# Activation parts and the work buffers behind them start 32 bytes higher in SBUF, at 96 instead of 64 modulo 256

## The chip, the cores and the metric

One NeuronCore of a Trainium2 chip runs one program that holds two transformer-like blocks in a row. The metric is the device time of one execution in microseconds. Three timed executions of the kernel before stand against the same number of the changed one.

## The reference, cut to what matters

The input x is 256 tokens by 1024 features, with a context of the same shape. The first block scales and shifts a normalised x and ctx by learned modulations, runs gated linear attention in both directions with states carried from the context, projects back, and adds a gated feed-forward layer of width 2816. The second block projects its modulated input to a gated delta rule branch (8 heads, chunks of 64) and a chunked band attention branch (16 heads), merges them through gates, and ends with layer norms and another gated feed-forward layer with a short convolution. All of it is float32:

```python
hc = modulate(rms_norm(x, norm_g), shift, scale)
y = (silu(hc @ w_gate) * (hc @ w_up)) @ w_out          # first block's feed-forward, width 2816
proj = h @ w_in                                        # second block: 9232 columns
merged = gate_a * (o_a @ w_branch_a) + gate_b * (o_b @ w_branch_b)
x = layernorm(ALPHA * x + gate_t * (merged @ w_o), ln1_g, ln1_b)
```

Nearly all of the work is in such products of the 256 tokens with weight matrices of 1024 or 2816 rows.

## The kernel before, in words

The weights are laid out as 178 panels of 128 partitions x 2048 numbers. SyncE streams them in halves of 128x1024 through the six slots of `raw` (L140, issue at L295 to L298). A panel of kind "S" is multiplied on TensorE in three passes: ScalarE rounds a half of it to the upper part `w_hi` (`upper_half`, L946), VectorE subtracts that from the half to get the lower part `w_lo` (`lower_half`, L1460), four slots each. The activations are split in the same way into `act_hi` and `act_lo` (16 tiles of 128x256), and the hidden layer of the feed-forwards into `hidden_hi` and `hidden_lo` (22 tiles). Panels of other kinds are reduced on VectorE (L1493) or multiplied once by a padded vector (L451).

`three_pass` (L394 to L401, its matmul is L399) takes a weights pair and a moving pair and issues upper x upper, upper x lower, lower x upper, each with a load of 128 stationary columns and a stream of 256 (in two panels 512) moving columns:

```python
for p, (a, b) in enumerate(((a_hi, b_hi), (a_hi, b_lo), (a_lo, b_hi))):
    ins = pe.matmul(out_, a, b, start=start and p == 0, stop=stop and p == 2,
                    skip_group_check=True)
```

Here `a` is loaded as the stationary operand and `b` streams. A column panel (`quarter`, `panel`) loads slices of `w_hi`/`w_lo` and streams a 256-token tile of the activations, so each product reads 512 bytes of weights and 1024 bytes of activations in every partition. A token panel (`token_quarter`, for the values of both attentions) swaps the roles: 128 tokens of the activations are loaded and 256 columns of the weights stream. `project_hidden` does the same as a column panel from the hidden parts. In the trace's names the moving operand stands first: `panel_banks<-act_hi,w_hi` streams `act_hi`.

The order of work is written out by hand for each engine: a list of layers (`LAYERS`) gives the stream of panels, and for the delta rule and the band attention a table (`FILL`) says how many quarters of panels TensorE puts between their steps. Semaphores tie the engines: `landed` (DMA), `upper_ready`, `parts_ready`, `multiplied`, `panel_evacuated`. SyncE's queue waits for the release of a slot of `raw` before it issues the next load.

SBUF is allotted in the order of the declarations, each buffer at a multiple of 32 bytes. The start of each, modulo 256: `raw`, `w_hi`, `w_lo` and `x_t` 128 (the first of them at 16512), `columns` 128, `ident`, `ones`, `twice_diag` and `c_wide` 0, `mod_cols` 0, `rs` 160, `w_beta_a` 96, then at L169

```python
sb("act_home", [P, 48])
with ExitStack() as scope:
    hhi = sb("act_hi", [P, 16, T], F32R, scope)
    hlo = sb("act_lo", [P, 16, T], F32R, scope)
```

`act_home` starts at 128 modulo 256, is used by nothing and takes 192 bytes, so that `act_hi` starts at 64 modulo 256. All buffers behind it have sizes that are multiples of 256 bytes up to the last, so `act_lo`, `band_q`, `band_k` (which lie over the same place later), the work areas `gla_work`, `mix_work` and `ffn_work` with all their parts of 256 or more numbers, `hidden_hi` and `hidden_lo` start at 64 too. Every tile of 256 columns and every weight slice of 128 columns steps by a multiple of 256 bytes, so within a product the start modulo 256 is that of its buffer.

Of the kernel before, what the change touches and what calls it, by code (L numbers as in the profile page):

```python
# [21 lines left out]
P = 128  # L22
# [96 lines left out]
def two_blocks(nc, panels, x, ctx_x, columns, c_rows, w_glr, w_gate, w_beta_a, head_rows, rel_bias, out):  # L119
# [3 lines left out]
    with ExitStack() as ctx:  # L123
        def sb(name, shape, dt=F32, scope=ctx):
            return scope.enter_context(nc.sbuf_tensor(name, shape, dt))
# [40 lines left out]
            return cols[:, COL[name] + i:COL[name] + i + n]  # L166


        sb("act_home", [P, 48])  # L169
        with ExitStack() as scope:  # L170
            hhi = sb("act_hi", [P, 16, T], F32R, scope)
            hlo = sb("act_lo", [P, 16, T], F32R, scope)
# [1970 lines left out]
```

How the kernel before makes its waits and increments, by code:

```python
        @block.sync  # L285
        def _(sp):
            for u in range(2 * len(stream)):
                if u >= RAW:
                    kind, i = stream[(u - RAW) // 2]
                    if kind != "R":
                        sp.wait_ge(S(RELEASE[kind]), 2 * i + u % 2 + 1)
                    else:
                        for g in range(4):
                            sp.wait_ge(S(f"rows{g}"), 2 * i + u % 2 + 1)
                sp.dma_start(raw[:, u % RAW], panels[u // 2][:, u % 2 * HALF:u % 2 * HALF + HALF])\
                    .then_inc(S(f"landed{u % RAW}"), 16)
            for k in (0, 2, 4, 6):
                sp.wait_ge(S("out_ready"), k + 2)
                sp.dma_start(out[:, k:k + 2], f_out[:, k:k + 2]).then_inc(S("out_stored"), 16)
            sp.wait_ge(S("out_stored"), 64)
# [2 lines left out]
        @block.gpsimd  # L303
# [3 lines left out]
            def step(ins):  # L307
                made[0] += 1
                ins.then_inc(S("constants"), 1)
                pool.wait_ge(S("constants"), made[0])
# [34 lines left out]
            assert made[0] == CONSTANTS, made[0]  # L345
            for g in range(4):
                for d in range(2):
                    pool.dma_start(wgp[32 * g + 16 * d:32 * g + 16 * d + 16, 512 * d:512 * d + 512], w_gate[d])\
                        .then_inc(S("gate_w_landed"), 16)
            pool.wait_ge(S("h1_lo"), KT)
            step(pool.memset(resets, 1.0))
            step(pool.memset(resets.rearrange("p (a b) -> p a b", b=T)[:, :, 0], 0.0))
```

## Time and profile before

| what | value |
|---|---|
| three timed executions | 1027.47, 1031.45, 1030.05 us; median 1030.05 |
| the profiled execution's own time | 1027.39 us |
| its span, first to last instruction | 1025.6 us |
| TensorE busy | 948.5 us (92%), 8438 matmuls |
| VectorE busy | 702.4 us (68%), 1112 instructions |
| ScalarE busy | 547.6 us (53%), 829 instructions |
| mean granted TensorE clock | 0.966 |
| HBM read | 194.43 MB, 191 GB/s over the span |

The span of the profiled execution is 1.8 us shorter than its own time. Busy times of TensorE are those of overlapping products, so the share says that something is always in flight, not how quickly products follow each other. The granted clock is the share of 2.4 GHz that TensorE was given; it is 1.0 or 0.5 in a stretch.

### The profile page before, as it was taken

The page shows a single profiled execution, that of the slowest core. Times are in us where ns is not written, and L with a number is a line of the kernel's source. Part 1 is how long each engine was busy: PE and PEld are TensorE (multiplying, and loading weights), DVE is VectorE, ACT ScalarE, POOL GpSimd, SP SyncE. Part 2 cuts the span into 40 slices and gives each one's busy share as a digit, 9 for nine tenths or more (in the row PEclk, how much of TensorE's full clock was granted, in tenths as well). Part 3 has the DMA queues.
Part 4 walks back from the last instruction along what each step waited for, and adds up shares of the span by engine and source line. Part 5 has one row for each costly group of instructions (what it writes and reads, how often), then busy time and mean ns, then how long its engine had stood idle before and what let it go on. Part 6 is the DMA issues. An engine that isn't in the chain of part 4 may idle for free.

```text
span 1025.6 us, 19911 instructions
## 1 busy us (share of the span) xinstructions
PE 948.5 (92%) x8438; PEld 895.5 (87%) x8438; DVE 702.4 (68%) x1112; ACT 547.6 (53%) x829; POOL 26.7 (3%) x71
## 2 busy tenths in 40 slices
PE   4699999979999998899899999989998699999995
PEld 1489999869999998799689998978998599999994
DVE  2659837677787775888784544456668689989744
ACT  2668232655544445665726335366764467766434
POOL 2100000000000000400100000000000000000000
PEclk9899999979999999899999999989999899999997
DMA  9825656537888887357324335544356635666921
GB/s 337 298 90 161 236 200 211 201 124 250 308 282 286 301 281 246 101 180 257 120 84 166 116 134 134 185 134 135 114 204 219 224 113 195 193 198 192 340 88 41
DMA packets 57401, 196.78 MB, mean 192 GB/s; under 512 B 6097, under 2 KB 10593, under 8 KB 57057
## 3 DMA queue, kind: packets, MB, share of 16 engines
q1 hardware_dynamic: 51840, 187.72, 54.2%
q10 hardware_dynamic: 5216, 7.53, 2.8%
q8 instruction: 66, 1.08, 0.4%
q0 software_dynamic: 256, 0.26, 0.1%
q14 instruction: 23, 0.18, 0.1%
HBM read 194.43 MB, written 1.06 MB: 191 GB/s over the span
## 4 chain that ended last, share of the span: by engine, by line
PE 74%; DVE 16%; ACT 5%; issue 2%; DMA 1%; ACTq 0%; SPq 0%; DVEq 0%
PE panel_banks L399 62%; DVE w_lo L1460 4%; DVE mix_work L1802 3%; PE work_banks L768 2%; ACT w_hi L946 2%; DMA raw<-in_panels 1%; DVE raw L1493 1%; PE work_banks L596 1%; PE work_banks L697 1%; DVE gla_work L1577 1%; PE panel_banks L451 1%; PE work_banks L739 1%; PE work_banks L556 1%; PE work_banks L529 1%; PE work_banks L851 1%
## 5 line engine op out<-in xcount | busy, mean ns | idle before, releaser
L399 PE MATMUL panel_banks<-act_hi,w_hi 128*128 128x256 f32 (+1 forms) x1600 | 461.3, 288 | 24.1 <-DVE w_lo L1460 9.3
L399 PE MATMUL panel_banks<-act_lo,w_hi 128*128 128x256 f32 (+1 forms) x1600 | 452.4, 283 | 0.0
L399 PE MATMUL panel_banks<-act_hi,w_lo 128*128 128x256 f32 (+1 forms) x1600 | 452.4, 283 | 0.0
L1460 DVE TENSOR_TENSOR w_lo<-raw,w_hi 128x1024 fp32r<-128x1024 f32 x260 | 315.4, 1221 | 140.6 <-ACT w_hi L946 138.5
L946 ACT ACTIVATE w_hi<-raw 128x1024 fp32r<-128x1024 f32 x260 | 272.4, 1055 | 159.9 <-PE panel_banks L399 116.7
L399 PEld LDWEIGHTS panel_banks<-act_hi,w_hi 128*128 128x128 f32 x1600 | 306.0, 191 | 37.3 <-issue 20.0
L399 PEld LDWEIGHTS panel_banks<-act_lo,w_hi 128*128 128x128 f32 x1600 | 306.1, 191 | 2.1 <-issue 0.5
L399 PEld LDWEIGHTS panel_banks<-act_hi,w_lo 128*128 128x128 f32 x1600 | 306.0, 191 | 1.6
L399 PE MATMUL panel_banks<-hidden_hi,w_hi 128*128 128x256 f32 x352 | 98.3, 279 | 2.7 <-ACT hidden_hi L1165 2.7
L399 PE MATMUL panel_banks<-hidden_lo,w_hi 128*128 128x256 f32 x352 | 98.0, 278 | 0.0
L399 PE MATMUL panel_banks<-hidden_hi,w_lo 128*128 128x256 f32 x352 | 98.0, 278 | 0.0
L1493 DVE CUSTOM_DVE_ANT_0 raw<-raw,c_wide 128x1024 f32<-128x1024 f32 x80 | 94.6, 1219 | 1.0 <-DMA raw<-in_panels 0.8
L399 PEld LDWEIGHTS panel_banks<-hidden_hi,w_hi 128*128 128x128 f32 x352 | 66.1, 188 | 3.3 <-ACT hidden_hi L1165 1.8
L399 PEld LDWEIGHTS panel_banks<-hidden_lo,w_hi 128*128 128x128 f32 x352 | 66.8, 190 | 0.0
L399 PEld LDWEIGHTS panel_banks<-hidden_hi,w_lo 128*128 128x128 f32 x352 | 66.1, 188 | 0.0
L399 PE MATMUL panel_banks<-w_hi,act_hi 128*128 128x256 f32 x192 | 55.4, 288 | 2.2 <-DVE w_lo L1460 2.2
L399 PE MATMUL panel_banks<-w_hi,act_lo 128*128 128x256 f32 x192 | 54.4, 283 | 0.0
L399 PE MATMUL panel_banks<-w_lo,act_hi 128*128 128x256 f32 x192 | 54.3, 283 | 0.0
L2036 DVE SCALAR_TENSOR_TENSOR ffn_work<-panel_banks,columns,ffn_work 128x255 f32<-128x255 f32 (+1 forms) x88 | 38.4, 477 | 13.3 <-ACT ffn_work L1409 12.6
L399 PEld LDWEIGHTS panel_banks<-w_hi,act_hi 128*128 128x128 f32 x192 | 36.8, 192 | 3.0 <-DVE w_lo L1460 2.4
L596 PE MATMUL work_banks<-ffn_work,ones 128*128 128x256 f32 x64 | 23.2, 506 | 16.3 <-DVE ffn_work L1689 8.1
L399 PEld LDWEIGHTS panel_banks<-w_lo,act_hi 128*128 128x128 f32 x192 | 36.7, 191 | 0.3 <-issue 0.2
(268 smaller groups left out, 962.6 us busy)
## 6 DMA issues: line engine op xcount, KB each, us to landing
raw<-in_panels SPq DMA_DIRECT2D x356, 512.0 KB, 5.1
mix_work<-delta_rows ACTq DMA_DIRECT2D x2, 1024.0 KB, 14.0
x_t<-in_x ACTq DMA_DIRECT2D x1, 1024.0 KB, 9.0
gla_work<-in_ctx_x ACTq DMA_DIRECT2D x1, 1024.0 KB, 13.9
mix_work<-in_rel_bias ACTq DMA_DIRECT2D x1, 1024.0 KB, 8.7
out_x<-ffn_work SPq DMA_DIRECT2D x4, 256.0 KB, 2.5
mix_work<-in_rel_bias ACTq DMA_DIRECT2D x1, 768.0 KB, 13.7
c_wide<-in_c_rows ACTq DMA_DIRECT2D x1, 512.0 KB, 4.3
```

The source lines that it names most:

```text
L399: ins = pe.matmul(out_, a, b, start=start and p == 0, stop=stop and p == 2, skip_group_check=True)
L451: pe.matmul(PB[32 * g:32 * g + 32, a % TURNS, 0:256], cpad[:, 4 * h + g, :], raw[:, u % RAW, g * 256:g * 256 + 256], start=(h == 0), stop= ...
L529: ins = pe.matmul(MB[:, h, t * T:t * T + T], g_k3[:, 4 * d + h, t * P:t * P + P], g_q3[:, 4 * d + h, :], start=(d == 0), stop=(d == 1))
L556: ins = pe.matmul(MB[:, (h + 2) % 4, v * T:v * T + T], g_v[:, n, h * GDV + v * P:h * GDV + v * P + P], g_a[:, h, n, :], start=(n == 2 and ...
L596: ins = pe.matmul(MB[:, bank, 0:T], ones[:, 0:P], src[:, k, :], start=(k == 0), stop=(k == 6 + tiles - 1))
L697: ins = pe.matmul(MB[:, b, :], ones[:, 0:P], sq3[:, part * 8 + 2 * b:part * 8 + 2 * b + 2, :], start=True, stop=True)
L768: ins = pe.matmul(o, lhs[half, m, :], rhs[half, m, :], start=True, stop=True)
L946: act.activation(whi[:, v_ % PARTS, :], raw[:, u % RAW, :], ACT.Copy)\
L1460: dve.tensor_tensor(wlo[:, v_ % PARTS, :], raw[:, u % RAW, :], whi[:, v_ % PARTS, :].bitcast(F32), ALU.subtract)\
L1493: dve.tensor_tensor_reduce(raw[:, u % RAW, :], raw[:, u % RAW, :], cwide[:], 1.0, 0.0, ALU.mult, ALU.add, dst).then_inc(S("accumulated"), 1)
L1802: ins = dve.scalar_tensor_tensor(o, b[:, m * T:m * T + T - s], col("conv_a_2", 24 * (3 - s) + 2 * i + m), o, ALU.mult, ALU.add)
L2036: ins = dve.scalar_tensor_tensor(o, b[:, m * T:m * T + T - s], col("conv_ffn_2", 44 * (2 - s) + 22 * m + i), o, ALU.mult, ALU.add)
```

## The change

One line: the unused buffer ahead of the activation parts grows from 48 to 56 float32 numbers in each partition, 192 to 224 bytes. `act_hi`, `act_lo` and every buffer behind them start 32 bytes higher, at 96 modulo 256. `raw`, `w_hi`, `w_lo`, `x_t`, the constants, `rs` and the small columns stay where they are. The last buffer still ends inside SBUF. No instruction changes but for addresses.

```diff
@@ -166,7 +166,7 @@
             return cols[:, COL[name] + i:COL[name] + i + n]
 
 
-        sb("act_home", [P, 48])
+        sb("act_home", [P, 56])
         with ExitStack() as scope:
             hhi = sb("act_hi", [P, 16, T], F32R, scope)
             hlo = sb("act_lo", [P, 16, T], F32R, scope)
```

## Rows read from the trace of the kernel before

**Rows 1.** Spans and granted clock of the cores.

```profile
...
core 0: 1025.6 us, clock 0.966
...
```

**Rows 2.** The page's chain that ended last, its two lines.

```profile
...
PE 74%; DVE 16%; ACT 5%; issue 2%; DMA 1%; ACTq 0%; SPq 0%; DVEq 0%
PE panel_banks L399 62%; DVE w_lo L1460 4%; DVE mix_work L1802 3%; PE work_banks L768 2%; ACT w_hi L946 2%; DMA raw<-in_panels 1%; DVE raw L1493 1%; PE work_banks L596 1%; PE work_banks L697 1%; DVE gla_work L1577 1%; PE panel_banks L451 1%; PE work_banks L739 1%; PE work_banks L556 1%; PE work_banks L529 1%; PE work_banks L851 1%
...
```

**Rows 3.** Groups by shape, TensorE: count, busy us, mean ns, idle before.

```profile
...
L399 PE MATMUL panel_banks<-act_hi,w_hi 128*128 128x256 f32 x1568 | 447.6, 285 | 18.0 <-DVE act_lo L1659 6.5 <-DVE act_lo L1661 5.8 <-DVE w_lo L1460 3.2
...
L399 PE MATMUL panel_banks<-hidden_hi,w_hi 128*128 128x256 f32 x352 | 98.3, 279 | 2.7 <-ACT hidden_hi L1165 2.7
...
L399 PE MATMUL panel_banks<-w_hi,act_hi 128*128 128x256 f32 x192 | 55.4, 288 | 2.2 <-DVE w_lo L1460 2.2
...
```

**Rows 4.** Stretches, L399 alone: bounds, length, PE busy (count), clock, DMA share, GB/s.

```profile
...
73.00:91.00 18.00, 18.00 (x160) 1.00 0.41 129
228.50:345.00 116.50, 116.50 (x1031) 1.00 0.84 285
347.50:404.50 57.00, 57.00 (x505) 1.00 0.85 285
426.00:447.00 21.00, 21.00 (x188) 1.00 0.44 143
449.00:483.00 34.00, 34.00 (x302) 1.00 0.76 244
826.00:944.00 118.00, 118.00 (x1044) 1.00 0.57 186
...
```

**Rows 5.** The same view, six other stretches.

```profile
...
98.50:117.00 18.50, 18.50 (x159) 1.00 0.51 162
125.50:135.50 10.00, 10.00 (x87) 1.00 0.98 367
153.50:163.50 10.00, 10.00 (x87) 1.00 0.57 182
751.00:778.00 27.00, 27.00 (x231) 1.00 0.67 223
781.00:790.00 9.00, 9.00 (x79) 1.00 0.62 184
951.00:1008.00 57.00, 57.00 (x486) 1.00 0.51 177
...
```

**Rows 6.** Timeline of TensorE, 657.1 to 667 us: start, length, instruction.

```profile
...
657.23 0.28 PE L399 MATMUL panel_banks<-w_lo,act_hi 128*128 128x256 f32 x1
...
662.64 0.28 PE L399 MATMUL panel_banks<-w_hi,act_lo 128*128 128x256 f32 x1
662.76 0.28 PE L399 MATMUL panel_banks<-act_hi,w_hi 128*128 128x256 f32 x1
...
663.00 0.28 PE L399 MATMUL panel_banks<-act_hi,w_lo 128*128 128x256 f32 x1
...
666.97 0.28 PE L399 MATMUL panel_banks<-act_lo,w_hi 128*128 128x256 f32 x1
```

**Rows 7.** Groups by shape, VectorE: count, busy us, mean ns, idle before.

```profile
...
L1703 DVE TENSOR_TENSOR x_t<-x_t,ffn_work 128x512 f32<-128x512 f32 x8 | 5.5, 692 | 0.3
...
L1709 DVE TENSOR_TENSOR ffn_work<-ffn_work,rs 128x512 f32<-128x512 f32 x8 | 5.5, 684 | 1.8 <-ACT rs L961 1.8
...
```

**Rows 8.** Groups by shape, ScalarE, within rs and within the GLA buffer.

```profile
...
L961 ACT ACTIVATE gla_work<-gla_work 128x512 f32<-128x512 f32 x2 | 1.3, 629 | 0.1
...
L961 ACT ACTIVATE rs<-rs 128x512 f32<-128x512 f32 x1 | 0.6, 629 | 0.0
...
```

**Rows 9.** DMA issues: KB each, median us to landing.

```profile
...
gla_work<-in_ctx_x ACTq DMA_DIRECT2D x1, 1024.0 KB, 13.9
...
```

**Rows 10.** Stretch from 221 to 228 us, TensorE, all lines.

```profile
...
221.00:228.00 7.00, 6.10 (x27) 0.51 0.33 116
...
```

## Prediction, written before the changed kernel ran

> **What bounds the kernel now.** I read the summary of the core first: a span of 1025.6 us at a mean granted clock of 0.966 [rows 1]. The profiled execution took 1027.39 us, so 1.8 us lie outside the span; the median of the three timed executions is 1030.05 us, 2.7 us above it. The sum below is a difference, made on the profiled execution, and I add it to the median. Then the chain of waits: 74% of it is TensorE, and one line, the three-pass product L399, has 62% by itself [rows 2]. VectorE has 16% and DMA 1%, so a slower element-wise operation would have to be much slower to count, and a slower product counts at once. Then the groups of L399 by shape: one row for each pass, and three passes alike. The 256-column products number 3 x 1568 with the activation parts streaming, 3 x 352 with the hidden parts streaming and 3 x 192 with the weight panels streaming, 6336 in all [rows 3].
>
> The mean duration of one product (278 to 288 ns) says little, since products overlap. What matters is the spacing of their starts. I took it from the table of stretches: length of a long unbroken stretch divided by the number of L399 products in it, less 2 for those already in flight at its left edge. Six stretches give 364.5 us for 3218 products, 113.3 ns each [rows 4]. Six others give 131.5 us for 1117 products, 117.7 ns each [rows 5]. The granted clock is 1.00 in every one of them, so this is not the clock. Nothing lies between: **the product stream has two cadences, 4.4 ns (3.9%) apart**, and each holds for hundreds of products once entered, whatever ScalarE, VectorE and DMA do beside it (DMA busy share 0.41 to 0.85 in the first set, 0.51 to 0.98 in the second).
>
> Do addresses have to do with it? Two facts pull apart. The hidden parts stream at 113.3 ns from 347.5 to 404.5 us and at 117.8 ns from 951 to 1008 us, from the same buffers against the same weight slots [rows 4, 5], so the addresses alone don't choose. But at 662.7 us the cadence changes with no stall at all, exactly where the operands swap roles: 46 steps of a token panel take 5.41 us (117.6 ns; weights stream from 128 modulo 256, activations are loaded from 64), and from 663.00 us 35 steps of a column panel take 3.97 us (113.4 ns; the roles and addresses swapped) [rows 6]. The token stretches that begin at 125.5 and 153.5 us are at the longer cadence too [rows 5]. So the pair of streams seems to matter, as well as how a run begins.
>
> **The change, part by part.** No instruction, wait or transfer is added, removed or reordered; 32 bytes more are set aside in each partition and every later buffer starts 32 bytes higher.
>
> Step 1, element-wise work on moved buffers: cost 0. The rs buffer starts at 160 modulo 256, so it already lies 32 past a multiple of 64, as all moved buffers will. With it as a source a 128x512 product takes 684 ns, and an addition of the same size between buffers at multiples of 64 takes 692 ns [rows 7]. ScalarE takes 629 ns for 128x512 within rs and 629 ns within the GLA work buffer [rows 8]. The largest VectorE and ScalarE groups read and write raw, w_hi and w_lo, which don't move. Bound: the VectorE pair differs by 8 ns, 1.2%; VectorE has 16% of the chain, 4% of it in L1460, which doesn't move [rows 2]; 1.2% of the other 12% of 1025.6 us is 1.5 us either way.
>
> Step 2, DMA: cost 0. The panel transfers write raw, which stays. Of the few that write moved buffers, the largest before the first product is the context load, 13.9 us from issue to landing [rows 9]. It starts at no multiple of 256 before or after. Bound: 1 us either way.
>
> Step 3, the products, is the only one with weight. In a column panel the streamed operand starts at 64 and the loaded one at 128 modulo 256, a difference of -64; after the change it is -32. In a token panel it is +64 and becomes +32. The trace has no product of this kind with a difference of 32, so I bound its cost by the two cadences that it does show. The twelve stretches hold 4335 of the 6336 products. The other 2001 lie in short runs of both kinds; I take them as half and half. That makes some 4219 at the short cadence and 2117 at the long. If every product went at the long one: 4219 x 4.44 ns = +18.7 us. If every one went at the short: 2117 x 4.44 = -9.4 us. Between these ends I take the value nearest to the rows in hand, the same mix: for operands that only change their start, the hidden parts show both cadences at one and the same address, so the start of a run chooses more than the address does, and the waits at which runs start are left as they are. A mix also drifts from execution to execution (one stretch of 118 us at the other cadence is 1042 x 4.44 = 4.6 us), which is as large as the spread of the three times, 4.0 us.
>
> A rule to weigh here. The row shows two spacings for one shape at one clock [rows 4 to 6]. The Trainium skill, "TensorE: Matmul & The Clock Gate", in its step-by-step part, gives TensorE two independent read ports into SBUF and says that loading the next weights takes no read bandwidth from the running matmul. By that rule no relative address could matter and step 3 would be exactly 0. The role swap without a stall speaks against it as the whole story, so both ends stay in the range.
>
> Step 4, the clock: cost 0. The granted clock of 0.966 over 1025.6 us means 34.9 us lost, in stretches at 1.2 GHz behind idle time of TensorE, as from 221 to 228 us, where it is 0.51 and only 27 matmuls ran [rows 10]. One such stretch more or less is 3.4 us; the waits that cause them aren't changed. If the cadence shifts, one may come or go: 3 us either way.
>
> Sum: 0, so 1030 us.
>
> **The rivals.** (a) The long cadence takes over. Mechanism: the streamed operand and the load behind it come to fetch from the same part of SBUF at the same time, in column panels, above all in the long runs of the two gated layers (228.5 to 345 and 826 to 944 us), now at 113.3 ns. All of them: 1030 + 18.7 = 1049 us; half, 1039 us. It decides from 1160 of the 4219 products on (5.15 us / 4.44 ns). For: token panels, with a pair of other relative address, are never seen at the short cadence in the long stretches. Against: moving from -64 towards 0 is not moving to their +64.
>
> (b) The short cadence takes over, by the same dependence with the other sign; the runs from 751 and from 951 us would show it first. All of them: 1030 - 9.4 = 1021 us; the column panels of those two runs alone (229 and 484 products), 3.2 us, would still be inside the noise. For: the long cadence holds a third of the products, so there is something to win. DMA doesn't stand in the way: at 113.3 ns the stretch from 228.5 us runs with DMA busy at 0.84 and no stall.
>
> (c) A start 32 bytes off a multiple of 64 costs every product one step of the same size more, beyond what the trace shows: 6336 x 4.44 = +28 us, 1058 us. For: neither stream starts there today. Against: the streamed operand starts at 128 in token panels and at 64 in others, and 117.7 ns is seen for both, so which boundary a row straddles has cost nothing so far. The Trainium skill, "SBUF — State Buffer", Specifications, gives SBUF lines of 16 bytes, which a shift by 32 leaves aligned; no run here shows that line size.
>
> (d) That the change doesn't do what it says: the buffer before has 192 bytes and ends where the activation parts begin, the new one has 224, a multiple of the 32 to which buffers are placed, so I give it nothing.
>
> **How the numbers follow.** A measurement of this kernel can tell about 0.5%, 5.2 us. The same mix within that: 0.40. (a) by more than 5.2 us: 0.28. (b) by more than that: 0.24. (c): 0.08. So faster 0.24, same 0.40, slower 0.36. The range: below, all at the short cadence less 1 to 2 us for steps 1, 2 and 4, 1020; above, all at the long one, 1049. It leaves out (c) and little at the edges of (a) and (b). The likeliest case alone lies between 1026 and 1034.
>
> **What would show each step right or wrong.** In the changed kernel's table of stretches, 228.5 to 345 us and 826 to 944 us should again hold some 1031 and 1044 products: 992 and 1005 would be (a). The runs that begin near 751 and 951 us should show 117.7 ns, or 113.3 for (b); any third spacing is (c) or something not thought of. Token panels at 113.3 ns would show that the pair of addresses decides. The duration rows of VectorE and ScalarE on moved buffers should stand within 8 ns of today's, and the waits of TensorE for VectorE should keep their size. The prediction is wrong if the mix changes by more than 1160 products, or if time moves with the mix unchanged.

## The result, and the profile after

The changed kernel takes 1044.22 us, the median of four runs (1043.44 to 1044.69), against 1030.64 us of the kernel before in four (1027.47 to 1031.45). The ratio is 1.0142 with a 95% interval of 1.0119 to 1.0166: **slower by 1.4%**, nearly three times what a measurement can tell. The forecast was no change. The profiled execution took 1044.23 us with a span of 1042.5 us, 16.9 us over that of [rows 1]; the difference of the medians is only 13.6 us, because the execution profiled before was one of the quicker ones.

The summary of the core, and the two lines of the chain of waits of the changed kernel:

```profile
...
core 0: 1042.5 us, clock 0.967
...
```

```profile
...
PE 83%; DVE 10%; ACT 4%; DMA 1%; issue 1%; SPq 0%; ACTq 0%; DVEq 0%
PE panel_banks L399 71%; DVE w_lo L1460 2%; PE work_banks L768 2%; DMA raw<-in_panels 1%; DVE raw L1493 1%; PE work_banks L596 1%; ACT w_hi L946 1%; PE work_banks L739 1%; PE work_banks L697 1%; PE work_banks L556 1%; PE work_banks L529 1%; PE work_banks L851 1%; PE work_banks L796 1%; ACT gla_work L984 0%; DVE act_lo L1472 0%
...
```

The granted clock is the same within 0.001. TensorE has 83% of the chain where it had 74% [rows 2], and L399 71% where it had 62%; VectorE's share fell from 16% to 10%. The chain points at the products but doesn't measure the loss: the gain of L399 in it is some 100 us, six times the 16.9 us, so the chain has also taken another path, through TensorE where it went through VectorE before.

The groups that answer to [rows 3]: with the same counts, the two that stream activations and hidden parts are 4 and 3 ns longer in the mean, the one that streams weights is unchanged.

```profile
...
L399 PE MATMUL panel_banks<-act_hi,w_hi 128*128 128x256 f32 x1568 | 452.7, 289 | 18.5 <-DVE act_lo L1661 6.6 <-DVE act_lo L1659 6.5 <-DVE w_lo L1460 2.9
...
L399 PE MATMUL panel_banks<-hidden_hi,w_hi 128*128 128x256 f32 x352 | 99.2, 282 | 2.3 <-ACT hidden_hi L1165 2.3
...
L399 PE MATMUL panel_banks<-w_hi,act_hi 128*128 128x256 f32 x192 | 55.3, 288 | 2.3 <-DVE w_lo L1460 2.3
...
```

The spacing of the products in long unbroken stretches, read as in [rows 4, 5]: length divided by the count less 2. First the column and hidden panels (columns: bounds, length, busy time of L399 and count, granted clock, DMA share, GB/s):

```profile
...
75.00:118.00 43.00, 43.00 (x367) 1.00 0.46 150
232.00:352.00 120.00, 120.00 (x1016) 1.00 0.81 272
356.00:412.00 56.00, 56.00 (x475) 1.00 0.82 280
438.00:457.00 19.00, 19.00 (x163) 1.00 0.49 152
460.00:494.00 34.00, 34.00 (x290) 1.00 0.72 239
838.00:955.00 117.00, 117.00 (x990) 1.00 0.57 179
...
```

These hold 389 us and 3289 products, 118.3 ns each, among them all the stretches that ran at 113.3 ns before. The first of them ends in a token panel, from 109 us on. Now the stretches that ran at 117.7 ns before, column and hidden panels:

```profile
...
748.00:790.00 42.00, 42.00 (x357) 1.00 0.57 185
792.00:800.00 8.00, 8.00 (x70) 1.00 0.53 183
968.00:1024.00 56.00, 56.00 (x475) 1.00 0.53 175
...
```

106 us and 896 products, 118.3 ns again. And three token stretches:

```profile
...
128.00:138.00 10.00, 10.00 (x88) 1.00 1.01 382
155.00:165.00 10.00, 10.00 (x87) 1.00 0.52 162
656.00:666.00 10.00, 10.00 (x88) 1.00 0.75 245
...
```

The first and the third hold 20 us and 172 products, 116.3 ns; the starts themselves give 116.7 ns there, the difference being the count at the edges of so short a window. The second, 10 us and 85 products, is at 117.7 ns (117.8 by the starts). **The two cadences of column panels have become one in this execution**, 118.3 ns, whatever came before a run (but for one short run of 32 products at 120.0 ns). Token panels went the other way: of their 576 products about three quarters are at 116.7 ns and one quarter still at 117.7.

The rest of the profile stands still. The groups on moved buffers that answer to [rows 7] and [rows 8]:

```profile
...
L1703 DVE TENSOR_TENSOR x_t<-x_t,ffn_work 128x512 f32<-128x512 f32 x8 | 5.5, 692 | 0.3
...
L1709 DVE TENSOR_TENSOR ffn_work<-ffn_work,rs 128x512 f32<-128x512 f32 x8 | 5.5, 685 | 1.8 <-ACT rs L961 1.8
...
```

```profile
...
L961 ACT ACTIVATE gla_work<-gla_work 128x512 f32<-128x512 f32 x2 | 1.3, 629 | 0.1
...
L961 ACT ACTIVATE rs<-rs 128x512 f32<-128x512 f32 x1 | 0.6, 629 | 0.0
...
```

```profile
...
gla_work<-in_ctx_x ACTq DMA_DIRECT2D x1, 1024.0 KB, 14.3
...
```

What the 16.9 us are made of can be counted from the starts of all 256-column products of L399 in the two traces. Steps of at most 130 ns (a step is the time from one start to the next), in which TensorE had nothing to wait for: 6113 before with a mean of 114.9 ns, 6128 after with 118.2 ns. The longer spacing is worth 6128 x 3.33 = 20.4 us, and 15 more steps fall into this class, 1.7 us. Longer steps, with a wait in them or at 1.2 GHz, went from 64.1 to 58.7 us: some 4 us less in waits and some 1.5 us less at the lower clock. All other matmuls stayed at 244.6 and 244.5 us: 20.4 + 1.7 - 5.4 - 0.1 = 16.6 us.

### The profile page after: what moved, and what is told of

Read it like the earlier page. It is cut to its first block, busy times and chain, and to the rows that moved or that the text cites. A ratio compares the mean times of both kernels' runs of the same rounds, so it can differ in the third digit from the quotient of the medians.

```text
span 1042.5 us, 19911 instructions
## 1 busy us (share of the span) xinstructions
PE 965.5 (93%) x8438; PEld 914.3 (88%) x8438; DVE 702.6 (67%) x1112; ACT 547.9 (53%) x829; POOL 26.9 (3%) x71
## 4 chain that ended last, share of the span: by engine, by line
PE 83%; DVE 10%; ACT 4%; DMA 1%; issue 1%; SPq 0%; ACTq 0%; DVEq 0%
PE panel_banks L399 71%; DVE w_lo L1460 2%; PE work_banks L768 2%; DMA raw<-in_panels 1%; DVE raw L1493 1%; PE work_banks L596 1%; ACT w_hi L946 1%; PE work_banks L739 1%; PE work_banks L697 1%; PE work_banks L556 1%; PE work_banks L529 1%; PE work_banks L851 1%; PE work_banks L796 1%; ACT gla_work L984 0%; DVE act_lo L1472 0%
## 5 line engine op out<-in xcount | busy, mean ns | idle before, releaser
L399 PE MATMUL panel_banks<-act_hi,w_hi 128*128 128x256 f32 (+1 forms) x1600 | 466.7, 292 | 25.7 <-DVE w_lo L1460 10.1
L399 PE MATMUL panel_banks<-act_lo,w_hi 128*128 128x256 f32 (+1 forms) x1600 | 458.4, 286 | 0.0
L399 PE MATMUL panel_banks<-act_hi,w_lo 128*128 128x256 f32 (+1 forms) x1600 | 458.0, 286 | 0.0
L399 PEld LDWEIGHTS panel_banks<-act_hi,w_hi 128*128 128x128 f32 x1600 | 306.5, 192 | 38.5 <-issue 20.4
L399 PEld LDWEIGHTS panel_banks<-act_lo,w_hi 128*128 128x128 f32 x1600 | 306.8, 192 | 2.2 <-issue 0.5
L399 PEld LDWEIGHTS panel_banks<-act_hi,w_lo 128*128 128x128 f32 x1600 | 306.6, 192 | 1.6
L399 PE MATMUL panel_banks<-hidden_hi,w_hi 128*128 128x256 f32 x352 | 99.2, 282 | 2.3 <-ACT hidden_hi L1165 2.3
L399 PE MATMUL panel_banks<-hidden_hi,w_lo 128*128 128x256 f32 x352 | 98.9, 281 | 0.0
L399 PE MATMUL panel_banks<-hidden_lo,w_hi 128*128 128x256 f32 x352 | 98.9, 281 | 0.0
L399 PEld LDWEIGHTS panel_banks<-hidden_hi,w_hi 128*128 128x128 f32 x352 | 66.3, 188 | 2.9 <-ACT hidden_hi L1165 1.7
L399 PEld LDWEIGHTS panel_banks<-hidden_lo,w_hi 128*128 128x128 f32 x352 | 66.3, 188 | 0.0
L399 PEld LDWEIGHTS panel_banks<-hidden_hi,w_lo 128*128 128x128 f32 x352 | 66.3, 188 | 0.0
L399 PE MATMUL panel_banks<-w_hi,act_hi 128*128 128x256 f32 x192 | 55.3, 288 | 2.3 <-DVE w_lo L1460 2.3
L399 PE MATMUL panel_banks<-w_lo,act_hi 128*128 128x256 f32 x192 | 54.3, 283 | 0.0
L399 PE MATMUL panel_banks<-w_hi,act_lo 128*128 128x256 f32 x192 | 54.1, 282 | 0.0
L399 PEld LDWEIGHTS panel_banks<-w_hi,act_hi 128*128 128x128 f32 x192 | 36.8, 191 | 3.1 <-DVE w_lo L1460 2.5
L1409 ACT ACTIVATE ffn_work<-panel_banks,columns 128x256 f32<-128x256 f32 x44 | 22.5, 561 | 31.6 <-PE panel_banks L399 31.6
## 6 DMA issues: line engine op xcount, KB each, us to landing
gla_work<-in_ctx_x ACTq DMA_DIRECT2D x1, 1024.0 KB, 14.3
```

What stands on the lines that cost most here:

```text
L1409: ins = act.activation(f_u[:, i % 2, m, :], b[:, m * T:m * T + T], ACT.Identity, scale=col("conv_ffn_2", 88 + 22 * m + i), bias=col("b_con ...
```

## The experiments

The theory after the result, called R: which cadences are possible is set by the distance between the address from which the moving operand streams and that from which the stationary operand is loaded, modulo 256. Its rival A: a row that starts 32 bytes off a multiple of 64 costs more to stream. A third possibility is that the work buffers, not the products, carry the loss.

### Everything 32 bytes up

```diff
+        sb("low_home", [P, 8])
         raw = sb("raw", [P, RAW, HALF])
```

> Every buffer 32 bytes up, raw and the weight parts too, so every distance between two buffers is that of the kernel before and every start is 32 past a multiple of 64. Theory R (the distance between the streamed and the loaded operand, modulo 256, sets the cadence): column panels show 113.3 and 117.8 ns as before, time 1027 to 1033 us. Theory A (a streamed row that starts off a multiple of 64 costs more): 118.3 ns throughout, 1044 us or more.

Measured: 1028.31 us (10 runs) against 1028.48 us of the kernel before (19 runs), ratio 1.001 (0.9986 to 1.0035). The stretches, column panels first, then the two hidden products:

```profile
...
250.00:330.00 80.00, 80.00 (x708) 1.00 0.86 290
860.00:930.00 70.00, 70.00 (x620) 1.00 0.61 197
365.00:395.00 30.00, 30.00 (x267) 1.00 0.87 297
970.00:1000.00 30.00, 30.00 (x257) 1.00 0.34 116
...
```

80 us / 706 and 70 us / 618 are 113.3 ns; the hidden products ran at 113.2 and 117.6 ns, the same two in the same order as in [rows 4, 5]. Every moved operand of the changed kernel starts at 96 here too, and nothing is lost. A falls.

### Only the weight parts moved

```diff
+        sb("w_home", [P, 56])
         whi = sb("w_hi", [P, PARTS, HALF], F32R)
         wlo = sb("w_lo", [P, PARTS, HALF], F32R)
+        sb("w_end", [P, 8])
         xt = sb("x_t", [P, KT, T])
```

> Activations and everything behind them stay at 64, only w_hi and w_lo go from 128 to 96, so the distance stream minus load in column panels is -32 as in the changed kernel, with the streamed row at a multiple of 64. Theory R: 118.3 ns throughout, 1044 us. Theory A: the streams of column panels keep their start, so 113.3 and 117.8 ns, 1030 us; only token panels (streams of the weights) get longer, by at most 576 products, 3 us.

Measured: 1044.46 us (4 runs, against the same 19), ratio 1.0164 (1.0131 to 1.0197).

```profile
...
250.00:330.00 80.00, 80.00 (x678) 1.00 0.83 281
365.00:395.00 30.00, 30.00 (x256) 1.00 0.83 268
860.00:930.00 70.00, 70.00 (x594) 1.00 0.58 187
...
```

80 us / 676, 30 us / 254 and 70 us / 592 are 118.3, 118.1 and 118.2 ns. The activations lie where they lay in the kernel before, and the whole loss is there. With the experiment ahead of it, this shows that it is the distance and not the start of either operand.

### The parts of the change by themselves

Only the activation parts at 96:

```diff
-        sb("act_home", [P, 48])
+        sb("act_home", [P, 56])
...
         bk = sb("band_k", [P, KT, T])
+        sb("act_end", [P, 56])
```

> act_hi, act_lo (and band_q, band_k) at 96, the work areas and the hidden parts at 64. If the products alone carry the loss and each buffer by itself: column panels from act at 118.3 ns throughout, hidden products at 113.3 or 117.8 ns; the hidden products hold some 2.8 us of the loss, so 1041 us. If work buffers on ScalarE and VectorE carried it: near 1030 us.

Only what lies behind them at 96:

```diff
         bk = sb("band_k", [P, KT, T])
+        sb("act_end", [P, 8])
```

> act_hi, act_lo at 64 as before, the work areas and the hidden parts at 96. By the products alone: act panels at 113.3 and 117.8 ns, hidden products at 118.3 ns, 1031 to 1034 us. If work buffers carried the loss: 1041 us or more.

Measured: 1042.16 us for the first (4 runs), ratio 1.0149 (1.0116 to 1.0181), and 1029.99 us for the second (10 runs), 1.0025 (0.9995 to 1.0054), which is no difference that these runs can tell (1031 to 1034 us were expected). First the one with only the activations moved, then its complement, with two column stretches and the hidden ones (both hidden products for the first version, the first of them for the second):

```profile
...
250.00:330.00 80.00, 80.00 (x669) 1.00 0.82 271
860.00:930.00 70.00, 70.00 (x594) 1.00 0.59 187
365.00:395.00 30.00, 30.00 (x267) 1.00 0.86 283
970.00:1000.00 30.00, 30.00 (x257) 1.00 0.82 290
...
```

```profile
...
250.00:330.00 80.00, 80.00 (x708) 1.00 0.85 289
860.00:930.00 70.00, 70.00 (x620) 1.00 0.60 195
365.00:395.00 30.00, 30.00 (x256) 1.00 0.84 288
...
```

In the first, column panels run at 119.9 and 118.2 ns and the hidden products at 113.2 and 117.6; in the second, column panels at 113.3 and the hidden product at 118.1. The loss follows each buffer into its own products, and work buffers carry none that these runs can tell.

The first shows two things more. Its activations and weight parts lie at the very addresses of the changed kernel, and yet a run of 1034 products goes at 120.0 ns where the changed kernel has 118.3: a distance of -32 has two levels as well, and the expectation of 118.3 ns throughout missed one of them. And its hidden parts, with 32 + 224 bytes more ahead of them, lie 256 bytes further from both weight parts than in the kernel before; the first hidden product still runs at 113.3 ns and the second at 117.7. So for these products an offset of 256 changes nothing, which is what lets distances be counted modulo 256.

### Six other places for the activations

All as the change, with another size of the buffer ahead, so that everything behind it starts at 192, 160, 128, 0, 224 and 32 modulo 256:

```diff
-        sb("act_home", [P, 48])
+        sb("act_home", [P, 16])
```

That is the one for 192. The numbers are 8 for 160, 32 for 0, 24 for 224 and 40 for 32; for 128 the line is left out.

> Stream minus load is +64 in column panels, the distance that token panels have in the kernel before, and -64 in token panels. Theory R with the roles not mattering: column panels at 117.8 ns throughout, token panels at 113.3 or 117.8 ns; about 1048 us less what slack absorbs, 1043 to 1048 us. If the role (which operand is the weight panel) matters and not the distance: column panels keep 113.3 ns somewhere, near 1030 us.

> Stream minus load +32 in column panels, as token panels have in the changed kernel; -32 in token panels. Theory R: column panels at 116.7 ns (some at 117.8), token panels at 118.3 ns; 1038 to 1046 us. A theory by which any start 32 off a multiple of 64 costs the same: 118.3 ns in both, 1044 us.

> Distance 0 in both kinds of panel: the layout with no buffer ahead of the activations. Theory R gives no value for a distance not yet seen, but the same set of cadences in both kinds. If nearness of the two starts is what costs, it is at or above 118.3 ns and 1044 us or more; if the cost has its peak at -32, between, 1030 to 1044 us.

> Distance 128, half the period, in both kinds of panel. Theory R: the same set of cadences in both kinds. If the period is 128 rather than 256, it is that of distance 0. If nearness costs, this is the best place: 113.3 ns throughout, 1021 to 1025 us.

> Distance stream minus load +96 in column panels, -96 in token panels, the one pair of distances not yet seen, with its mirror in the next run. Theory R with a period of 256 demands only that this run and its mirror show the same cadences with column and token panels swapped; going by the neighbours (+64: 117.8, 128: 118.7) I expect 117.8 to 118.7 ns in column panels, 1038 to 1043 us.

> Distance -96 in column panels, +96 in token panels. Theory R: mirror of the run before. By the neighbours (-64: 113.3 or 117.8, 128: 118.7 or 120.0) between them: 1030 to 1043 us. If it is 113.3 ns throughout, this is the version to keep, 1021 us.

The stretch from 250 to 330 us, column panels, in each of them, in that order:

```profile
...
250.00:330.00 80.00, 80.00 (x682) 1.00 0.82 279
...
```

```profile
...
250.00:330.00 80.00, 80.00 (x688) 1.00 0.84 284
...
```

```profile
...
250.00:330.00 80.00, 80.00 (x669) 1.00 0.82 278
...
```

```profile
...
250.00:330.00 80.00, 80.00 (x677) 1.00 0.81 274
...
```

```profile
...
250.00:330.00 80.00, 80.00 (x669) 1.00 0.80 275
...
```

```profile
...
250.00:330.00 80.00, 80.00 (x676) 1.00 0.83 278
...
```

From the starts, the means over all runs of more than 12 products between waits give this map. Distance is stream minus load modulo 256, column panels count the hidden products in, and both kernels of the change are rows of it. Levels are rounded to a third of a nanosecond; those that hold over 100 products are listed, the most frequent first, and means within 0.4 ns of a level are counted to it. (At distance 0, runs of 23 to 29 products have means of 119.3 to 119.5 ns, which I take for the edge of short runs.)

| distance | column panels, ns | token panels at the same distance, ns | time with column panels there, us | ratio to before (95%) |
|---|---|---|---|---|
| -64 (before) | 113.3, 117.7 | 113.3, 117.7 (act at 192) | 1028 to 1031 | 1 |
| -32 (the change) | 118.3; also 120.0 (only act at 96) | 118.3 (act at 160) | 1044.2 | 1.0142 (1.0119 to 1.0166) |
| 0 | 120.0 | 120.0 | 1047.9 | 1.0175 (1.0133 to 1.0217) |
| +32 (act at 160) | 116.7, 117.7 | 116.7, 117.7 (the change); also 120.0 (only act at 96) | 1038.0 | 1.0096 (1.0071 to 1.012) |
| +64 (act at 192) | 117.7, 113.3 | 117.7 (before) | 1038.5 | 1.0084 (1.0054 to 1.0113) |
| +96 (act at 224) | 120.0 | 120.0 (act at 32) | 1049.1 | 1.0215 (1.0148 to 1.0282) |
| 128 (act at 0) | 118.7, 120.0 | 118.7 | 1041.5 | 1.0112 (1.0081 to 1.0142) |
| -96 (act at 32) | 118.7, 117.3, 120.0 | 117.3, 118.7 (act at 224) | 1041.1 | 1.0137 (1.0107 to 1.0168) |

The cadences of each place come from one profiled execution, and the times of the six places from two runs each, but for act at 160 with nine. Of those nine the profiled one was the quickest by far, 1030.88 us at a granted clock of 0.976, against 1036.22 to 1041.09 us for the other eight, so its levels needn't be those behind the 1038.0 us.

The two columns of cadences contradict each other in no row, though the roles of weights and activations are swapped between them (in a row, one list may have a level that the other lacks, but every level of the shorter list is in the longer). So the set of cadences goes with the distance; 0 and 128 differ, so the period isn't 128. My guesses from neighbours were poor: I expected +96 between 117.8 and 118.7 ns, +64 throughout at 117.8 ns with 1043 us or more (it has runs at 113.3 and took 1038.5), and, if nearness costs, 128 as the best place. Distance 0 was the second worst, and no place throughout at 113.3 ns was found. The distance of the kernel before is the best of the eight by time.

The times differ by less than the cadences. At distance 0 the products take 31 us more than in the kernel before (6172 steps of 119.9 ns against 6113 of 114.9, taken at the same count), but the span is only 19 us longer: the steps with a wait or at 1.2 GHz shrink from 64.1 to 47.4 us, and the granted clock is 0.974 where it was 0.966.

### The passes apart

Two versions move one part of a pair only. The three passes load w_hi, w_hi and w_lo and stream act_hi, act_lo and act_hi. The trace of the kernel before shows what lies beside what:

```profile
...
250.01 0.28 PE L399 MATMUL panel_banks<-act_lo,w_hi 128*128 128x256 f32 x1
250.01 0.19 PEld L399 LDWEIGHTS panel_banks<-act_hi,w_lo 128*128 128x128 f32 x1
...
```

The load of w_lo for the third pass begins with the stream of act_lo in the second. That is the pairing which the expectations here use: the lower pair is act_lo with w_lo. But a load lasts 0.19 us and a product 0.28 us, as recorded, while the starts are 0.113 us apart, so every stream has more than one load beside it, and the records don't tell which of them meets it.

Only act_hi to 96, which streams in two passes of three:

```diff
-        sb("act_home", [P, 48])
+        sb("act_home", [P, 56])
...
+            sb("lo_home", [P, 56], F32, scope)
             hlo = sb("act_lo", [P, 16, T], F32R, scope)
...
+        sb("under_home", [P, 56])
         sb("under_lo", [P, KT, T])
```

> Only act_hi goes to 96 (with band_q over it); act_lo, the hidden parts and the work areas stay at 64. act_hi streams in two passes of three, each beside a load of w_hi. Theory R pass by pass: (2 x 118.3 + 113.3) / 3 = 116.7 ns for the mean of three, hidden products as before; 1037 us. If one pair is enough to hold all three passes: 118.3 ns and 1042 us.

Only w_lo, to 0:

```diff
+        sb("lo_home", [P, 32])
         wlo = sb("w_lo", [P, PARTS, HALF], F32R)
+        sb("lo_end", [P, 32])
         xt = sb("x_t", [P, KT, T])
```

> Only w_lo moves, from 128 to 0: act_lo streams beside the load of w_lo at a distance of +64, the other two passes keep -64. Theory R pass by pass: one pass in three changes from a pair that allows 113.3 ns to one that mostly shows 117.8, so the mean of three passes is 114.8 where it was 113.3, or 117.8; 1033 to 1037 us. If the three passes lock as a whole, one cadence for all, new or old.

Measured: 1039.08 us for the first (2 runs), ratio 1.0118 (1.0082 to 1.0153), and 1022.41 us for the second (6 runs), **0.9943 (0.9916 to 0.9969), faster than both kernels**. First act_hi alone at 96, then w_lo at 0:

```profile
...
250.00:330.00 80.00, 80.00 (x681) 1.00 0.82 279
...
```

```profile
...
250.00:330.00 80.00, 80.00 (x708) 1.00 0.87 289
860.00:930.00 70.00, 70.00 (x620) 1.00 0.62 195
365.00:395.00 30.00, 30.00 (x267) 1.00 0.86 302
970.00:1000.00 30.00, 30.00 (x267) 1.00 0.25 80
...
```

With act_hi alone the mean is 117.8 ns, and the three steps of a group differ in the starts: 120.0 and 119.1 ns from the two passes that stream act_hi, 114.2 ns from the one that streams act_lo. The pass-by-pass picture had 118.3, 118.3 and 113.3 ns, 116.7 in the mean, and its size is missed by 1.1 ns. Nor are unequal steps a sign of split parts: with all activations at 0, where the distance is 128 in every pass, the steps of a run of 1040 products are 117.0, 123.0 and 120.0 ns by pass. With w_lo at 0 I expected a loss, and all four stretches run at 113.2 to 113.3 ns, the second hidden product too, which ran at 117.7 ns in the kernel before and in every version that kept its layout. The long cadence is gone from column panels (short runs there have means of up to 115.6 ns); token panels keep 117.7 ns.

A repeat and three more versions followed, since it was open whether this was luck and which pair carries it. The repeat is the same kernel as that with w_lo at 0. The second is the changed kernel (act_home of 56) with w_lo at 64:

```diff
+        sb("lo_home", [P, 48])
         wlo = sb("w_lo", [P, PARTS, HALF], F32R)
+        sb("lo_end", [P, 16])
         xt = sb("x_t", [P, KT, T])
```

The third moves act_lo to 192 in place of w_lo, with the buffers that lie over it later:

```diff
+            sb("lo_home", [P, 32], F32, scope)
             hlo = sb("act_lo", [P, 16, T], F32R, scope)
...
+        sb("under_home", [P, 32])
         sb("under_lo", [P, KT, T])
         bk = sb("band_k", [P, KT, T])
+        sb("act_end", [P, 32])
```

The fourth is the third with w_lo at 0 as well; x_t and the constants go up by 128 there, and act_hi stays at 64. Only what differs from the third is shown, with the line of the kernel before marked as removed:

```diff
+        sb("wlo_home", [P, 32])
         wlo = sb("w_lo", [P, PARTS, HALF], F32R)
...
-        sb("act_home", [P, 48])
+        sb("act_home", [P, 16])
```

> The kernel with w_lo at 0 once more, with more rounds, beside the kernels of this call: column and hidden panels at 113.3 ns throughout, 1021 to 1025 us, 0.4 to 0.8% under the kernel before. If its lead was luck of the mix, nothing will be left of it: within 0.3%.

> The changed kernel with w_lo moved from 128 to 64, so that the lower pair (act_lo streams, w_lo is loaded) has a distance of +32 and the upper pairs keep -32: 118.3, 118.3 and some 116.7 ns, 117.8 ns in the mean, 1042 us. If splitting the lower pair from the upper ones is what gains by itself, whatever the distances, it falls well below: 1035 us or less.

> The lower pair at +64 by way of act_lo instead of w_lo; hidden parts and work areas stay at 64. If the distance in the lower pair decides, wherever it comes from: act panels at 113.3 ns throughout, hidden ones 113.3 or 117.8 as before, 1023 to 1027 us. If it was the place of w_lo itself: act panels at both cadences, 1028 us.

> w_lo at 0 and act_lo at 192. Which load lies beside a stream? If that of the product behind it (act_lo streams while w_lo is loaded): all three pairs of act panels are at -64 as in the kernel before, 113.3 or 117.8 ns by stretch, and the hidden ones (hidden_lo at 64) 113.3 throughout; 1025 to 1029 us. If that of the product itself (act_lo with w_hi, act_hi with w_lo): two pairs in three at +64, act panels near 117.8 ns throughout, 1036 us.

Measured, in that order: 1023.32 us in 12 runs (1021.08 to 1027.12) against 1028.03 in 23 (1023.78 to 1035.8), ratio 0.9954 (0.9929 to 0.9979); 1044.14 us in 2, 1.0149 (1.0081 to 1.0217); 1036.0 us in 8, 1.0065 (1.0033 to 1.0098); 1046.71 us in 2, 1.0174 (1.0105 to 1.0243).

```profile
...
250.00:330.00 80.00, 80.00 (x708) 1.00 0.85 293
860.00:930.00 70.00, 70.00 (x620) 1.00 0.61 195
970.00:1000.00 30.00, 30.00 (x267) 1.00 0.33 110
...
```

```profile
...
250.00:330.00 80.00, 80.00 (x679) 1.00 0.83 279
...
```

```profile
...
250.00:330.00 80.00, 80.00 (x681) 1.00 0.84 279
365.00:395.00 30.00, 30.00 (x267) 1.00 0.84 295
...
```

```profile
...
250.00:330.00 80.00, 80.00 (x664) 1.00 0.80 271
365.00:395.00 30.00, 30.00 (x267) 1.00 0.85 289
...
```

The gain of w_lo at 0 is no luck: again 113.3 ns in all three stretches, and both intervals lie below 1. The fourth version confirms it for the hidden products, which see the same layout there and ran at 113.3 ns there (113.4 in the second hidden product, by the starts). But the explanation that I had is not enough. Moving act_lo instead of w_lo gives the same distances in the same pairs, and column panels run at 117.8 ns throughout. Moving both should have given back the distances of the kernel before if a load lies beside the stream of the product ahead of it, or 117.7 ns if beside its own; it gave 120.8 ns, neither. And in the second, the mean stayed at 118.2 ns, where 117.8 was expected. So one distance describes the cadence only while upper and lower parts start at the same place modulo 256; with the three passes at different places something more matters, which these runs don't resolve. One difference between moving w_lo and moving act_lo is open too: the 256 bytes of the first edit lie ahead of the activations, so act_hi is 256 bytes further from w_hi there, and in the second edit it isn't. For hidden products 256 bytes made no difference; for split activation parts no run has it alone.

## Why the prediction was wrong

Bounds and method held. That the stream of three-pass products bounds the kernel, that it has two cadences, and that steps 1, 2 and 4 are worth nothing is what the profile after shows: the VectorE pair takes 692 and 685 ns after 692 and 684, the context load 14.3 us after 13.9, the clock is the same within 0.001. The version with everything but the activation parts moved, at 1.0025, shows the same for all of step 1 together. DMA did not stand in the way. The mix that I took, 4219 short and 2117 long, has a mean of 114.8 ns, and the count over all starts gave 114.9.

**What failed is step 3**, where I kept the same mix, for the reason that "the hidden parts show both cadences at one and the same address, so the start of a run chooses more than the address does". The first half is true, and it holds in the versions with the distance unchanged: the first hidden product ran at 113.3 and the second at 117.7 ns with everything 32 bytes up, as before. But the conclusion does not follow. The start of a run chooses between the cadences that a distance allows; the distance says which those are, and at -32 there is no 113.3: the stretches that had it went to 118.3 ns, which is 3.33 ns more for the mean product and 20.4 us where I had put 0. The role swap at 662.7 us in [rows 6] was the evidence for that, in the trace and in the text, and I gave it to the range and not to the value. The token stretches of [rows 5] also misled me in one respect: I read them as token panels being unable to run at the short cadence, and with the activations at 192 both signs of 64 show both.

Rival (a) had the right sign, place and nearly the price: the long runs of the two gated layers and everything else at one long cadence. I took 117.7 ns and 18.7 us for it from the rows in hand; the level turned out as 118.3 ns, and the products cost 20.4 us more in the profiled execution. What was missing from its sum is what comes back: 5.4 us less in steps with a wait or at 1.2 GHz. That the longer products cover these waits is the likely reason, and not shown apart. Its argument against itself, that going from -64 towards 0 isn't going to +64, was sound reasoning about the wrong quantity: the map rises at once on the way to 0. Rival (c) falls with the first experiment: with everything at 32 past a multiple of 64 the time is that of before. The 1044 us lie within the range, since its upper end was rival (a) in full; the likeliest case's own range, 1026 to 1034, does not hold them.

The rule that I weighed, from the Trainium skill, "TensorE: Matmul & The Clock Gate", step-by-step part, that loading the next weights takes no read bandwidth from the running matmul because each has its own read port, would leave the relative address without effect. The first two experiments show an effect for this kind of product: with the same instructions and only the distance between the two operands changed, the spacing goes from 113.3 to 118.3 ns. So load and stream aren't independent here; what they share, a port or something else, no run shows.

The spread of the kernel before, 4.0 us in the first four runs and 12 us in 23 later ones (1023.78 to 1035.8), against 1.3 us of the changed kernel in four, fits a mix that varies between executions at -64 and less so at -32, where the two levels are 1.7 ns apart and not 4.4. That is argued, not shown: only one execution of each was profiled.

## What to carry to other kernels

Where a kernel is bound by back-to-back products, divide the length of an unbroken stretch by the count and look for a few discrete spacings before looking at waits; an unused buffer of a few bytes ahead of one operand moves all of them, and it costs one run to try a place. Two levels at one address don't show that the address is without effect; compare the set of levels, not one value. Where stationary and moving operands come from separate buffers, try their distance in steps of 32 bytes over 256, and the parts of a split operand separately: that found 0.5% here that no placing of all activations together gave.

## What the runs showed of the hardware

- At a granted clock of 1.00, products of 128x128 by 256 columns in float32r with a fresh load each follow each other at 113.3, 116.7, 117.3, 117.7, 118.3, 118.7 or 120.0 ns, by the distance of the two operands modulo 256, as long as all parts of an operand start at the same place. Most of these levels were seen to hold over a thousand products, at DMA shares from 0.5 to 0.9.
- The distance is signed: in the map, -96 gives mostly 118.7 and 117.3 ns and +96 gives 120.0; -32 gives mostly 118.3 and +32 mostly 116.7. Swapping the roles of the buffers at one signed distance gives no level that contradicts this.
- What picks between the levels of one distance is open. As a rule it is settled when a run of products begins: the first hidden product ran at 113.3 and the second at 117.7 ns in all five kernels whose hidden parts are at -64 from both weight parts, and in the kernel before, the runs of 23 products between the steps of the band attention alternate between 113.7 to 114.0 and 117.6 to 117.8 ns, 14 in a row. It isn't always so: with the activations at 192, one run of 96 token products goes from 113.3 to 117.8 ns in its middle with no wait. No run here varied it alone.
